# Hymba-style decoder layer, one Trainium2 core: the attention's row minima masked on VectorE, turned by one product per head and brought to rows by eight transfers

## The reference, cut to what matters

```python
# group A (NSA), 8 heads: three softmaxes over the same query, gated and summed
s_c = einsum(q, kc) * scale;  p_c = _masked_softmax(s_c, cmp_end <= t)        # compressed blocks
s_s = einsum(q, k_sel) * scale;  p_s = _masked_softmax(s_s, kpos <= t)        # all selected blocks: causal
s_w = einsum(q, k_w) * scale;  p_w = _masked_softmax(s_w, (0 <= rel) & (rel < WINDOW))   # WINDOW = 512
o = g0 * (p_c @ vc) + g1 * (p_s @ v_sel) + g2 * (p_w @ v_w)
# group B (forgetting attention), 8 heads: one causal softmax with a bias from the cumulated log forget gate
logits = einsum(q, k) * scale + (cum[q] - cum[k]);  p = _masked_softmax(logits, kpos <= t);  o = p @ v
```

## Time and profile before

| | us |
|---|---|
| median of 3 runs | 1574.29 (1573.68 to 1575.49) |
| the profiled execution's own time | 1571.68 |
| its span in the trace | 1570.0 |
| busy: TensorE products / weight loads | 1386.4 / 1165.6 |
| busy: VectorE / ScalarE / GpSimd | 761.8 / 630.2 / 150.8 |

### The profile page before, as it was taken

The page is one execution under the profiler, slowest core; times in us unless marked ns, Lnnn a source line. Parts: engine busy times, 40 slices in busy tenths (PEclk is TensorE's granted clock), DMA queues, the critical chain, the costliest instruction groups (busy, mean ns, idle before and its releaser), DMA issues. The chain is left out here.

```text
span 1570.0 us, 24161 instructions
## 1 busy us (share of the span) xinstructions
PE 1386.4 (88%) x7980; PEld 1165.6 (74%) x7981; DVE 761.8 (49%) x1242; ACT 630.2 (40%) x932; POOL 150.8 (10%) x146
## 2 busy tenths in 40 slices
PE   4999999836999999999979992899999999937996
PEld 3767879834999999888868872677777787725774
DVE  6633112235444444354344324758754676846552
ACT  6211120013333333454453220657644666744442
POOL 0000000004111112233100000000000000012000
PEclk9999999966999999999989995899999999977998
DMA  5122412045000011345023221969987798784421
GB/s 186 54 81 81 130 57 58 10 104 128 21 22 22 21 35 42 96 113 119 15 83 121 81 94 52 393 208 386 398 299 257 252 364 285 303 314 132 138 74 41
DMA packets 108053, 222.49 MB, mean 142 GB/s; under 512 B 14813, under 2 KB 41469, under 8 KB 107974
## 3 DMA queue, kind: packets, MB, share of 16 engines
q1 hardware_dynamic: 97014, 183.08, 35.6%
q0 software_dynamic: 7488, 27.27, 4.9%
q10 hardware_dynamic: 3472, 11.09, 1.8%
HBM read 176.56 MB, written 36.24 MB: 136 GB/s over the span
## 5 line engine op out<-in xcount | busy, mean ns | idle before, releaser
L1179 ACT ACTIVATE att_prob<-att_ps_s 128x512 f32<-128x512 f32 (+1 forms) x240 | 134.7, 562 | 246.3 <-PE att_ps_s L1106 201.5
L1228 DVE TENSOR_REDUCE att_mx<-att_ps_m 128x1 f32<-128x512 f32 (+3 forms) x256 | 132.9, 560 | 134.3 <-PE att_ps_m L1053 122.6
L1954 DVE TENSOR_TENSOR exp_g_lo<-exp_g_raw,exp_g_hi 128x1024 fp32r<-128x1024 f32 x128 | 148.0, 1218 | 41.9 <-ACT exp_g_hi L1866 41.9
L136 PE MATMUL moe_ps_g<-exp_g_hi,moe_xT_hi 128*128 128x512 f32 x336 | 137.7, 410 | 15.3 <-DVE exp_g_lo L1954 15.3
L1124 PE MATMUL att_ps_o<-tok_vsw,att_prob 128*128 128x65 f32 x1056 | 140.2, 274 | 0.0
L1866 ACT ACTIVATE exp_g_hi<-exp_g_raw 128x1024 fp32r<-128x1024 f32 x128 | 124.9, 1048 | 37.6 <-PE moe_ps_g L138 19.8
L137 PE MATMUL moe_ps_g<-exp_g_lo,moe_xT_hi 128*128 128x512 f32 x336 | 134.0, 399 | 0.0
L138 PE MATMUL moe_ps_g<-exp_g_hi,moe_xT_lo 128*128 128x512 f32 x336 | 133.9, 398 | 0.0
L1124 PEld LDWEIGHTS att_ps_o<-tok_vsw,att_prob 128*128 128x128 f32 x1056 | 131.3, 192 | 2.6 <-ACT att_prob L1179 0.5
L136 PE MATMUL prj_ps_w<-prj_hT_hi,prj_w_hi 128*128 128x512 f32 x256 | 102.9, 402 | 3.0 <-DVE prj_w_lo L406 3.0
L138 PE MATMUL prj_ps_w<-prj_hT_hi,prj_w_lo 128*128 128x512 f32 x256 | 100.1, 391 | 0.0
(11 more groups left out here) (348 smaller groups left out, 2904.4 us busy)
## 6 DMA issues: line engine op xcount, KB each, us to landing
exp_g_raw<-in_w_gate_e SPq DMA_DIRECT2D x128, 256.0 KB, 4.8
exp_g_raw<-in_w_up_e SPq DMA_DIRECT2D x128, 256.0 KB, 5.5
exp_d_raw<-in_w_down_e SPq DMA_DIRECT2D x64, 512.0 KB
y_rows<-moe_y ACTq DMA_DIRECT2D x21, 512.0 KB, 6.4
prj_w_raw<-in_w_in SPq DMA_DIRECT2D x16, 512.0 KB, 4.0
att_q_raw<-feat SPq DMA_DIRECT2D x32, 256.0 KB, 4.8
feat<-att_w_out POOLq DMA_DIRECT2D x14, 512.0 KB, 2.9
att_k_raw<-feat SPq DMA_DIRECT2D x24, 256.0 KB, 6.1
```

What stands on the lines that cost most here:

```text
L136: nc.tensor.matmul(out, a_hi, b_hi, start=first, stop=False)
L1179: nc.scalar.activation(prob[:, b % PT, 0:w], ps_s[:, b % ST, 0:w], ACT.Exp, scale=-1.0).then_inc(expd, 1)
L1228: last = nc.vector.tensor_reduce(mx[i % 2][:, col, q:q + 1], p[:, at:at + (kb - ka) * P], X, ALU.min)
L1954: nc.vector.tensor_tensor(g_lo[:, ch % GR], g_raw[:, ch], g_hi[:, ch % GR].bitcast(F32), ALU.subtract).then_inc(s_glo, 1)
```

## The change

VectorE adds the masks itself. Where a piece of the minima has a masked tile, its reduction becomes a `tensor_tensor_reduce` that adds the mask from `maskb` (SBUF, bfloat16) to the products in `ps_m` (PSUM), writes the sum back to `ps_m` and leaves the minimum in one column of `mx`. `maskb` is laid out anew so that every piece finds its masks, with zero tiles between, in one stretch; it grows by three tiles and is filled by four instructions instead of one. The 288 mask products of the minima and `mask_minimum` go; the banks of four pieces are reduced by four instructions instead of one. `mx` becomes a plain row of 40 columns, ordered by query tile, so that one product turns all minima of a head (24 columns to 24 rows in an NSA head, 8 in a FOX head) in place of eight; `rows_out` is one copy of 24 (8) rows of 128; and `rows(i)` is eight transfers, one per query tile, of 3 (1) rows of 128 from `mT` to `q_two`. The ring of `ps_m` has one place per head for the rows in place of two. The masks of the scores (line 1106) stay as they are.

```diff
-                steps.inc(nc.vector.tensor_copy(K["maskb"][:], c[:, K_DIAG:K_DIAG + (2 + NT) * P]))
+                steps.inc(nc.vector.tensor_copy(K["maskb"][:, M_FAR * P:(M_FAR + 1) * P], c[:, K_FAR:K_FAR + P]))
+                steps.inc(nc.vector.memset(K["maskb"][:, (M_FAR + 1) * P:M_DIAG * P], 0.0))
+                steps.inc(nc.vector.tensor_copy(K["maskb"][:, M_DIAG * P:(M_DIAG + 1) * P], c[:, K_DIAG:K_DIAG + P]))
+                steps.inc(nc.vector.tensor_copy(K["maskb"][:, M_CMP * P:], c[:, K_CMP:K_CMP + NT * P]))
...
 MINIMA = {
-    CAUSAL: ([(0, 0, 1, 0), (2, 0, 3, 0)], [(1, 0, 2, 0), (5, 4, 6, 1)], [(3, 0, 4, 0)], [(4, 0, 4, 0)], [(5, 0, 4, 0)],
-             [(6, 0, 4, 0)], [(7, 0, 4, 0)], [(4, 4, 5, 1), (6, 4, 7, 1)], [(7, 4, 8, 1)]),
-    NEAR: ([(0, 0, 1, 2), (2, 0, 3, 2)], [(1, 0, 2, 2)], [(3, 0, 4, 2)], [(4, 0, 4, 2)], [(5, 1, 5, 2)], [(6, 2, 6, 2)],
-           [(7, 3, 7, 2)], [(4, 4, 5, 3), (5, 5, 6, 3), (6, 6, 7, 3), (7, 7, 8, 3)]),
-    BLOCKS: ([(q, 0, 1, 4) for q in range(4)], [(q, 0, 1, 4) for q in range(4, 8)]),
+    CAUSAL: ([(0, 0, 1, 0), (2, 0, 3, 0)], [(1, 0, 2, 0), (5, 4, 6, 3)], [(3, 0, 4, 0)], [(4, 0, 4, 0)], [(5, 0, 4, 0)],
+             [(6, 0, 4, 0)], [(7, 0, 4, 0)], [(4, 4, 5, 3), (6, 4, 7, 3)], [(7, 4, 8, 3)]),
+    NEAR: ([(0, 0, 1, 1), (2, 0, 3, 1)], [(1, 0, 2, 1)], [(3, 0, 4, 1)], [(4, 0, 4, 1)], [(5, 1, 5, 1)], [(6, 2, 6, 1)],
+           [(7, 3, 7, 1)], [(4, 4, 5, 4), (5, 5, 6, 4), (6, 6, 7, 4), (7, 7, 8, 4)]),
+    BLOCKS: ([(q, 0, 1, 2) for q in range(4)], [(q, 0, 1, 2) for q in range(4, 8)]),
 }
...
+M_FAR, M_DIAG, M_CMP = 0, 4, 5
...
     if branch == BLOCKS:
-        return 2 + q
-    return 0 if q == kb else 1 if branch == NEAR and q == kb + WB else None
+        return M_CMP + q
+    return M_DIAG if q == kb else M_FAR if branch == NEAR and q == kb + WB else None
...
-        mx = [sc.sb(f"mx{s}", [P, 5, NT]) for s in range(2)]
-        mT = [sc.sb(f"mT{s}", [3, S], F32R) for s in range(2)]
+        mx = [sc.sb(f"mx{s}", [P, NT * 5]) for s in range(2)]
+        mT = [sc.sb(f"mT{s}", [3 * NT, P], F32R) for s in range(2)]
...
-            order = [("min", k, x) for k in range(HEADS) for x in [*range(len(minima[k])), "row0", "row1"]]
...
-            if x in ("row0", "row1"):
-                return min_copied, 2 * k + (1 if x == "row0" else 2)
+            if x == "rows":
+                return min_copied, k + 1
             return min_taken, min_first[k] + x + 1
...
+        def rows_in(i):
+
+            return 16 * NT * (i // QS + 1)
...
                 def rows(i):
-                    sp.wait_ge(min_copied, 2 * i + 2)
+                    sp.wait_ge(min_copied, i + 1)
                     if i < QS:
                         sp.wait_ge(row_set, 2 * i + 2)
-                    sp.dma_start(q_two[i % QS][R_MIN:R_MIN + rows_of(i), :].bitcast(F32),
-                                 mT[i % 2][0:rows_of(i), :].bitcast(F32)).then_inc(row_in[i % QS], 16)
+                    rows = rows_of(i)
+                    for q in range(NT):
+                        sp.dma_start(q_two[i % QS][R_MIN:R_MIN + rows, q * P:(q + 1) * P].bitcast(F32),
+                                     mT[i % 2][q * rows:(q + 1) * rows, :].bitcast(F32)).then_inc(row_in[i % QS], 16)
...
-                    out, at, first, masks = ps_m[:, place(i, m), :], 0, True, []
+                    out, at = ps_m[:, place(i, m), :], 0
                     keys = fox_keys[(i - NH) % QS][2] if br == FOX else operands(i, br)[0]
                     for q, ka, kb, _ in MINIMA[br][n]:
                         lhs = (q_two if br == FOX else q_one)[i % QS][:, q * P:(q + 1) * P]
-                        own = [(at + (k - ka) * P, mask_of(br, k, q)) for k in range(ka, kb)
-                               if mask_of(br, k, q) is not None]
-                        last = nc.tensor.matmul(out[:, at:at + (kb - ka) * P], lhs, keys[:, ka * P:kb * P], start=first,
-                                                stop=not own, skip_group_check=True)
-                        first = False
-                        masks += own
+                        last = nc.tensor.matmul(out[:, at:at + (kb - ka) * P], lhs, keys[:, ka * P:kb * P], start=at == 0,
+                                                stop=True, skip_group_check=True)
                         at += (kb - ka) * P
-                    if not masks and not behind:
-                        last.then_inc(min_scored, 1)
-                    return masks
-
-                def mask_minimum(i, m, masks, more=0):
-                    for at, col in masks:
-                        last = nc.tensor.matmul(ps_m[:, place(i, m), at:at + P], K["identb"][:],
-                                                K["maskb"][:, col * P:(col + 1) * P],
-                                                start=False, stop=True, skip_group_check=True)
-                    if masks:
-                        last.then_inc(min_scored, 1 + more)
-
-                def turn(i, half):
-                    if half == 0:
-                        pe.wait_ge(joined, i + 1)
-                    free = ring_before("min", i, f"row{half}")
+                    last.then_inc(min_scored, 1)
+
+                def turn(i):
+                    pe.wait_ge(joined, i + 1)
+                    free = ring_before("min", i, "rows")
                     pe.wait_ge(*free)
-                    for j in range(4):
-                        last = nc.tensor.transpose(ps_m[0:rows_of(i), place(i, f"row{half}"), j * P:(j + 1) * P],
-                                                   mx[i % 2][:, own_columns(i), 4 * half + j], ident)
-                    last.then_inc(min_turned, 1)
+                    rows = rows_of(i) * NT
+                    nc.tensor.transpose(ps_m[0:rows, place(i, "rows"), 0:P],
+                                        mx[i % 2][:, 0:rows],
+                                        ident).then_inc(min_turned, 1)
...
                         pe.wait_ge(two_in[i % QS], 16 * (i // QS + 1))
-                        pe.wait_ge(row_in[i % QS], 16 * (i // QS + 1))
+                        pe.wait_ge(row_in[i % QS], rows_in(i))
...
                 for m in range(len(minima[0])):
-                    mask_minimum(0, m, minimum(0, m))
-                turn(0, 0)
-                turn(0, 1)
+                    minimum(0, m)
+                turn(0)
                 mask_score(0, score(0))
                 for b in range(NB):
                     i = head_of(b)
                     left = score(b + 1) if b + 1 < NB else []
                     now, rows = share(i, b - (bank_end[i - 1] if i else 0))
-                    lacking = []
                     for m in now:
-                        lacking.append(minimum(i + 1, m, any(lacking)))
+                        minimum(i + 1, m)
                     mask_score(b + 1, left)
-                    for n, m in enumerate(now):
-                        more = list(itertools.takewhile(lambda x: not x, lacking[n + 1:]))
-                        mask_minimum(i + 1, m, lacking[n], len(more))
                     if rows:
-                        turn(i + 1, 0)
-                        turn(i + 1, 1)
+                        turn(i + 1)
                     weigh(b)
...
-                def rows_out(i, half):
-                    act.wait_ge(min_turned, 2 * i + half + 1)
+                def rows_out(i):
+                    act.wait_ge(min_turned, i + 1)
                     if i >= 2:
-                        act.wait_ge(row_in[(i - 2) % QS], 16 * ((i - 2) // QS + 1))
-                    nc.scalar.activation(mT[i % 2][0:rows_of(i), half * 512:(half + 1) * 512],
-                                         ps_m[0:rows_of(i), place(i, f"row{half}"), :], ACT.Copy).then_inc(min_copied, 1)
+                        act.wait_ge(row_in[(i - 2) % QS], rows_in(i - 2))
+                    rows = rows_of(i) * NT
+                    nc.scalar.activation(mT[i % 2][0:rows, :], ps_m[0:rows, place(i, "rows"), 0:P],
+                                         ACT.Copy).then_inc(min_copied, 1)
...
-                rows_out(0, 0)
-                rows_out(0, 1)
+                rows_out(0)
...
                     if share(i, j)[1]:
-                        rows_out(i + 1, 0)
-                        rows_out(i + 1, 1)
+                        rows_out(i + 1)
...
-                        dve.wait_ge(min_turned, 2 * i - 2)
+                        dve.wait_ge(min_turned, i - 1)
                     dve.wait_ge(min_scored, min_first[i] + m + 1)
-                    took, at, p = MINIMA[br][n], 0, ps_m[:, place(i, m), :]
-                    if len(took) == 4:
-                        last = nc.vector.tensor_reduce(mx[i % 2][:, took[0][3], took[0][0]:took[3][0] + 1],
-                                                       p.rearrange("p (n k) -> p n k", n=4), X, ALU.min)
-                    else:
-                        for q, ka, kb, col in took:
```

(39 more changed lines are left out.)

## The result

The changed kernel takes 1673.0 us (median of four runs) against 1574.2 us before: 1.062 times as long, 95% interval 1.060 to 1.064. The profiled execution has a span of 1668.2 us against 1570.0, so 98.2 us more. The forecast was slower, 1604 us in a range of 1558 to 1640: the direction was right, the size was a third of the measured one, and the time lies outside the range.

A forecast was written before the change was run, and what follows sets the result against it. TensorE was taken to bound nearly the whole attention. Mask products -14.3, turns -11.4, waits +39.1, clock +11.9 and head 0 +7.1 summed to +32.4 us on 1571.7, so 1604 us; overall range 1558 to 1640, the forecast's own 1580 to 1630.

The forecast's parts named there:

- The bound: Nearly the whole attention, 386.2 to 797.0 us: TensorE always busy at full clock, so its queue sets the time.
- Mask products and turns: TensorE in the full stretch: 260 mask products gone, 14.3 us less, and 105 turns gone, 11.4 us less.
- The waits: TensorE waits for the eight row transfers in heads 1 to 7 and 9 to 15: 39.1 us more.
- The clock: TensorE's clock falls at half of the 14 waits, 1.7 us lost each: 11.9 us more.
- VectorE: Masked reductions at single rate plus 0.1 us per read: 4.2 us more per NSA head, 0.8 per FOX, hidden behind TensorE.
- Rival B: VectorE becomes the bound, with masked reductions at twice the rate and 0.19 us per read: 1652 us, chance 0.08.
- Head 0: The first head, without cover: VectorE's 4.2 us, less 0.8 for turn and copy, plus 3.7 for transfers: 7.1 us more.
- A: Rival on SyncE's queue: the eight issues come 0.31 us apart, no fall of the clock; 1560 us, chance 0.20.
- C: Rival: issues 0.75 us apart, waits of 60.1 us, 14 clock falls costing 23.8; 1638 us, chance 0.10.
- the estimate of 1549 us: Side estimate from a sequencer's dispatch of about 50 ns per transfer: no wait of TensorE left, 1549 us.
- The rule against small transfers: Trainium skill's advice, cited against the eight row transfers: merge many small transfers into one, since small ones are mostly overhead.

The follow-up runs named there:

- e4: Changed kernel with mx ordered by row, so three transfers of rows in an NSA head and one in a FOX head replace eight; 1550.3 us, ratio 0.982.
- e3: Changed kernel with 13 idle products of 128x512 in front of TensorE's wait for the rows in heads 1 to 15; 1599.0 us, ratio 1.015.
- e5: Changed kernel with 13 idle products of 128x512 behind TensorE's wait for the rows in heads 1 to 15; 1667.3 us in one run.
- e2: Kernel before the change with only the masks of the minima moved to VectorE; eight turns and one transfer stay; 1562.8 us, ratio 0.992.
- e6: Changed kernel with 6 idle products in front of the wait for the rows in heads 1 to 15; 1659.6 us, ratio 1.051.
- e7: Kernel of e4 with idle products of 128x512 added in head 0 alone; 1546.2 us, ratio 0.983.

## Why the prediction was right or wrong

- **The bound.** Right: TensorE sets this stage; VectorE and ScalarE never held it up outside head 0.
- **Mask products and turns, -14.3 and -11.4.** Right: 2.39 us for each NSA head in e4, where they give 2.30.
- **The waits, +39.1.** Right in place, number and nearly in size: 14, of 2.96 us in NSA heads (forecast 2.57) and 2.83 to 2.97 in FOX heads (3.02), 41 us together. In NSA heads the issues stand further apart than the 0.62 us taken, 0.69; in FOX heads it is 0.62 (4.97 us for eight); the last landing and the release took 1.8 us as assumed: 461.55 + 7 x 0.69 + 1.8 = 468.2.
- **The clock, +11.9.** This is the step that failed, by some 71 us, in both of its factors. "I let it happen at half of the 14 waits": it happened at all 14 (bounds "none and all": at the upper one). And "some 3.3 us at half speed, 1.7 us lost" was carried over from the experts' stage, where 512-column products follow the wait. In the attention the low stretch is 10.2 or 13.7 us, 5 to 7 us lost each: TensorE is busy for 166 us of them, so 83 us are lost, 5.9 each, where the sum had 12. e3 shows the sum of it (74 us back when TensorE isn't idle, although head 8 and head 0 cost some 7 us more there), e5 that the length depends on what follows, as between the two stages. The range's upper end was built from "all 14 falls" at the borrowed 1.7 us, which is why it was too low; its own terms (0.7 us, all falls) give 1624, where the text says 1630. With 83 us for 11.9 the sum comes to 1675, near the measured time, with the waits 2 us too low and head 0 3 us too high.
- **VectorE.** Right: the single rate and a separate read. The changed kernel's rows by shape, from 378 to 885 us:

```profile
L1218 DVE CUSTOM_DVE_ANT_0 att_ps_m<-att_ps_m,tok_maskb 128x512 f32<-128x512 f32 x65 | 45.1, 702 | 35.4 <-PE att_ps_m L1049 34.5 <-DVE att_tmp L1258 0.3
...
L1218 DVE DVE_READ_ACCUMULATOR2_ANT att_mx<- 128x1 f32 x270 | 37.9, 140 | 0.0
...
L1218 DVE CUSTOM_DVE_ANT_0 att_ps_m<-att_ps_m,tok_maskb 128x128 f32<-128x128 f32 x131 | 35.5, 315 | 147.6 <-PE att_ps_m L1049 147.6
```

  702 ns for 512 columns against 688 for the plain reduction, and the accumulator's read is a row of its own of 140 ns. The Trainium skill says so (VectorE: DVE Perf Modes, "Two Vector instructions with no wait between them": an instruction with an accumulator output is two). The trace agrees, with 270 reads in these rows. Rival B, VectorE as the bound, has nothing for it: no turn waits for the join outside head 0, and e2, which has VectorE's new work without the eight transfers, is faster.
- **Head 0, +7.1.** Too high: from TensorE's first product to line 1091 it took 388.14 - 364.77 = 23.4 us against 381.89 - 362.53 = 19.4, so +4.0. VectorE's chain of 4.2 us more was only 0.6 (first product to turn 15.85 us against 15.22), since the read overlaps the next instruction (pieces of 128 columns start 0.25 us apart there, though each takes 0.32) and the join took 0.17 us in place of 1.49. In e2 and e4 head 0 also loses to a clock that is low for 13 us behind its wait, against 4.4 us before; the forecast did not have this, and the changed kernel doesn't show it (3.6 us).
- **Rivals A and C.** A (issues 0.31 us apart) is out, and with it the estimate of 1549 us: the issues on SyncE's queue were 0.62 to 0.69 us apart. The 50 ns behind that estimate stand in the Trainium skill (DMA: Bandwidth & Descriptors, "Anatomy of one DMA") for the path of GpSimd and not for SyncE's. C (0.75 apart) had all 14 falls right, but its waits of 60.1 us were too long against 41, and its 1638 us also carried the borrowed length of a fall.
- **The rule against small transfers** (the Trainium skill, DMA: Bandwidth & Descriptors, "Rules for kernel authors"): the trace agrees, and e4 gives its price here: 0.69 us of the issuing queue for each transfer, whether it carries 1.5 or 4 KB.

## What to carry to other kernels

Count transfers on a latency path by their issues and not by their bytes, and choose the layout so that the turn yields rows which one transfer can take whole: the idea of this change was sound (24 us faster with three transfers), and the way its last step was cut made it lose 99 us instead. And where a stage keeps TensorE full with narrow products, price a wait of a few microseconds with the clock at the low level until the stage's own work wins it back, read from a fall in that same stage; here the clock cost twice the wait itself (5.9 us against 2.9). Such a fall, of nearly 7 us, stood in head 0 of the trace of before (379 to 386 us).

## What the runs showed that was not expected

- TensorE busy without a gap can stay at the low clock: 10.2 or 13.7 us at each wait of 3 us, and once 58 us (e6). With 13 products of 512 columns behind the same wait it is 3.4 us in nine of 13 places (e5).
- Waits of 1.4 to 2.2 us were enough to bring the clock down at 9 of 14 changes of head, and the runs of that kernel lie 23 us apart (e6). The low level need not begin inside the wait: in e6 TensorE works again from 465.1 us on and the clock falls at 467.0. And a wait need not bring it: none of the other five in e6, not the one of 2.9 us in head 13 of e5, not one of 1.1 us in head 6 of e7. At which of them it falls, and why the stage once stayed low for 58 us, stays open.
- With head 0's mask products gone, where TensorE is not the bound, the clock is low without a break up to 396 us in e2 and 398 us in e4, and before only up to 372 and again from 379 to 386. In the changed kernel, which lacks them too, it is full from 392 us on, so the masks alone don't decide it. With 41 idle products in head 0 (e7) the median is 3.9 us lower, with overlapping runs.
